# Gate products of a recurrent layer: rounded halves and rests in place of plain float32

## The reference, cut to what matters

```
xb = xc.reshape(b, s, 16, 128)                            # xc: the convolution's output, 2048 wide
r = sigmoid(einsum('bshc,hce->bshe', xb, w_a) + b_a)      # one 128x128 matrix per block
i = sigmoid(einsum('bshc,hce->bshe', xb, w_x) + b_x)
log_a = -8.0 * r * softplus(-lam)
a = exp(log_a)
u = sqrt(-expm1(2.0 * log_a)) * (i * xb)
h[t] = a[t] * h[t-1] + u[t]                               # forward, and once more backward
y = (h_forward + h_backward) * silu(gate) @ w_out + x
```

## Time and profile before

| | |
|---|---|
| median of 3 runs | 2190.18 us (2187.08 to 2191.71) |
| profiled execution | 2186.75 us |
| its span in the trace | 2184.9 us, 29571 instructions |
| granted TensorE clock | 0.995 of full speed |
| recurrent layer, tall panels | 422.4 to 641.5 us |

### The profile page before, as it was taken

One profiled execution on the slowest core, in us unless ns is written; L12 is line 12 of the kernel. 1 busy time (PEld: TensorE's weight loads), 2 busy tenths in 40 slices (PEclk: granted clock), 3 DMA queues, 4 the chain that ended last, 5 costly groups with the idle time before them and its releaser, 6 DMA issues.

```text
span 2184.9 us, 29571 instructions
## 1 busy us (share of the span) xinstructions
PE 2123.9 (97%) x12238; PEld 1521.8 (70%) x12238; DVE 1211.1 (55%) x1983; ACT 855.5 (39%) x1385; POOL 221.1 (10%) x301
## 2 busy tenths in 40 slices
PE   7999999999999999999999999999999899999998
PEld 6868757877777777898888888888867433333333
DVE  3532972439888867875423466345443445544454
ACT  4325461468886544672332542334443111111112
POOL 2000000013331022562000000000001000000000
PEclk9999999999999999999999999999999999999999
DMA  7122112423322444201222221433446899999994
GB/s 249 59 74 93 46 39 83 127 87 97 97 77 94 164 127 154 92 22 41 94 80 97 97 97 40 135 108 123 135 174 243 330 420 420 420 420 420 421 420 194
DMA packets 115703, 366.60 MB, mean 168 GB/s; under 512 B 7952, under 2 KB 36944, under 8 KB 90352
## 3 DMA queue, kind: packets, MB, share of 16 engines
q1 hardware_dynamic: 105888, 329.34, 40.2%
q0 software_dynamic: 9168, 29.00, 3.9%
q10 hardware_dynamic: 512, 6.34, 0.7%
HBM read 358.44 MB, written 10.54 MB: 169 GB/s over the span
## 4 chain that ended last, share of the span: by engine, by line
PE 88%; DVE 8%; ACT 2%; issue 1%; DMA 0%; POOL 0%; SPq 0%; DVEq 0%; ACTq 0%; POOLq 0%
PE bank L956 39%; PE bank L1167 13%; PE bank L1711 10%; PE bank L1725 5%; PE bank L1733 3%; PE bank L1284 2%; PE bank L1180 2%; PE bank L1211 2%; DVE resid L3369 2%; PE bank L1276 1%; PE bank L1113 1%; PE bank L1701 1%; PE bank L1104 1%; DVE w_lo L2447 1%; PE bank L1073 1%
## 5 line engine op out<-in xcount | busy, mean ns | idle before, releaser
L2447 DVE TENSOR_TENSOR w_lo<-raw,w_hi 128x2048 fp32r<-128x2048 f32 x117 | 268.6, 2296 | 444.1 <-ACT w_hi L1842 443.9
L1842 ACT ACTIVATE w_hi<-raw 128x2048 fp32r<-128x2048 f32 x117 | 223.9, 1914 | 393.9 <-PE bank L956 357.5
L3369 DVE TENSOR_TENSOR resid<-bank,resid 128x512 f32<-128x512 f32 x244 | 151.1, 680 | 182.6 <-PE bank L1733 182.6
L956 PE MATMUL bank<-hT_hi,w_hi 128*128 128x512 f32 x512 | 199.9, 390 | 2.5 <-DVE y_lo L3065 2.3
L956 PE MATMUL bank<-hT_lo,w_hi 128*128 128x512 f32 x512 | 199.2, 389 | 0.0
L956 PE MATMUL bank<-hT_hi,w_lo 128*128 128x512 f32 x512 | 199.2, 389 | 0.0
L1711 PE MATMUL bank<-piece,xT 128*64 128x512 f32 x792 | 183.4, 592 | 0.0
L1167 PE MATMUL bank<-hT_hi,w_hi 128*128 128x512 f32 x432 | 173.9, 402 | 0.9 <-DVE hT_lo L2511 0.9
L1167 PE MATMUL bank<-hT_hi,w_lo 128*128 128x512 f32 x432 | 168.2, 389 | 0.0
L1167 PE MATMUL bank<-hT_lo,w_hi 128*128 128x512 f32 x432 | 168.1, 389 | 0.0
L1711 PEld LDWEIGHTS bank<-piece,xT 128*64 128x64 f32 x792 | 59.5, 137 | 118.8 <-issue 118.8
(11 more groups left out here) (625 smaller groups left out, 4166.8 us busy)
## 6 DMA issues: line engine op xcount, KB each, us to landing
piece<-expert_w_gate SPq DMA_DIRECT2D x52, 1024.0 KB, 19.0
piece<-expert_w_down SPq DMA_DIRECT2D x49, 1024.0 KB, 19.2
piece<-expert_w_up SPq DMA_DIRECT2D x47, 1024.0 KB, 20.6
raw<-w_in SPq DMA_DIRECT2D x40, 1024.0 KB, 5.1
raw<-even_w_in SPq DMA_DIRECT2D x18, 1024.0 KB, 5.2
raw<-odd_w_in SPq DMA_DIRECT2D x16, 1024.0 KB, 5.6
raw<-expert_w_gate SPq DMA_DIRECT2D x12, 1024.0 KB, 16.8
raw<-expert_w_up SPq DMA_DIRECT2D x12, 1024.0 KB, 18.9
```

Source lines behind the costliest of these rows:

```text
L956: mm = pe.matmul(out, st, mv, start=first and x == 0, stop=last and x == 2)
L1842: act.activation(split_to(m)[0][:], raw[n % RAW][:], ACT.Copy).then_inc(sem("hi_done"), 1)
L2447: dve.tensor_tensor(split_to(m)[1][:], raw[split_of[m] % RAW][:], f32(split_to(m)[0][:]), ALU.subtract).then_inc(sem("lo_done"), 1)
L3369: dve.tensor_tensor(r, psum[bank][:], r, ALU.add).then_inc(sem(name), 1)
```

## The change

The gates' operands are split into a rounded half and a rest, as those of the large products are, and each plain product becomes three products that add into the same bank. GpSimd makes the four tiles of a block: it copies `gate_w` and `xc` into tiles of the rounded type (128x512 each) and then subtracts these from the originals. There is one set of tiles. So GpSimd waits until the gates of the block before are done on TensorE. It splits block `b + 1` ahead of its products L814 of block `b`. TensorE's two waits (for VectorE's convolution and for the weights' landing) move to GpSimd, and TensorE waits for the subtractions instead.

```diff
+        "gate_hi": ("qkT_done", 3 * NT),
+        "gate_lo": ("qkT_act", 2 * NT),
...
+    gw_hi = nc.alloc_sbuf_tensor_at("gw_hi", [P, 2, 2, P], F32R, offset=free_at)
+    gw_lo = nc.alloc_sbuf_tensor_at("gw_lo", [P, 2, 2, P], F32R, offset=free_at + 2048)
+    xc_hi = nc.alloc_sbuf_tensor_at("xc_hi", [P, SEQ], F32R, offset=free_at + 4096)
+    xc_lo = nc.alloc_sbuf_tensor_at("xc_lo", [P, SEQ], F32R, offset=free_at + 6144)
...
+        def split_gate(blk):
+
+            pool.wait_ge(sem(f"gates_in{blk % 2}"), 32 * (blk // 2 + 1))
+            src = panels[pn["xr"][blk // 2]]
+            pool.wait_ge(sem("evac_dve"), src["at"] + blk % 2 + 1)
+            if blk:
+                pool.wait_ge(sem("gate_done"), 4 * blk)
+            pool.tensor_copy(gw_hi[:], gate_w[blk % 2][:]).then_inc(sem("gate_hi"), 1)
+            pool.tensor_copy(xc_hi[:], xc[:, blk % XC]).then_inc(sem("gate_hi"), 1)
+            pool.wait_ge(*after("gate_hi", 2 * blk + 2))
+            pool.tensor_tensor(gw_lo[:], gate_w[blk % 2][:], f32(gw_hi[:]), ALU.subtract).then_inc(sem("gate_lo"), 1)
+            pool.tensor_tensor(xc_lo[:], xc[:, blk % XC], f32(xc_hi[:]), ALU.subtract).then_inc(sem("gate_lo"), 1)
+
         gate_weights(0)
         gate_weights(1)
+        split_gate(0)
         for blk in range(RB):
+            if blk + 1 < RB:
+                split_gate(blk + 1)
             for it in (2 * blk, 2 * blk + 1):
                 pool.wait_ge(sem("gate_sig"), 2 * it + 2)
                 pool.tensor_tensor(ri[:, it % 8], ri[:, it % 8], xc[:, blk % XC], ALU.mult).then_inc(sem("ix"), 1)
...
         def gates(blk):
 
-            src = panels[pn["xr"][blk // 2]]
-            pe.wait_ge(sem("evac_dve"), src["at"] + blk % 2 + 1)
-            pe.wait_ge(sem(f"gates_in{blk % 2}"), 32 * (blk // 2 + 1))
+            pe.wait_ge(*after("gate_lo", 2 * blk + 2))
...
-                    pe.matmul(psum[n % 4][:], gate_w[blk % 2][:, g, d], xc[:, blk % XC], start=True, stop=True).then_inc(sem("gate_done"), 1)
+                    products = ((gw_hi, xc_hi), (gw_lo, xc_hi), (gw_hi, xc_lo))
+                    for x, (w, v) in enumerate(products):
+                        mm = pe.matmul(psum[n % 4][:], w[:, g, d], v[:], start=x == 0, stop=x == 2)
+                    mm.then_inc(sem("gate_done"), 1)
```

## The result

The changed kernel takes 2198.69 us (median of six runs, 2197.17 to 2200.55) against 2191.4 us for the kernel before in the same sequence (six runs, 2187.08 to 2191.9). The ratio is 1.0038, with a 95% interval of 1.0026 to 1.0049: 0.38% slower, 8.3 us, between 5.7 and 10.7; the two medians lie 7.3 us apart. The forecast was +4.1 us and 2194.3; the range to 2202 holds the time. The 64 runs of before that were made beside the experiments fall into two groups with none between them, 2186.1 to 2188.3 us at a granted clock of 0.995 to 0.997 and 2189.7 to 2192.2 us at 0.993 or 0.994, and the profiled execution of before (2186.75 us) is of the quicker one.

The account below looks back on a forecast made before the run. TensorE was taken to bound the kernel, VectorE 10% behind. VectorE's 18.5 us of losses less 13.6 of waits and head start delay `rp_lo` 4.9 us, the projection 4.1: median 2194.3 us, range 2183 to 2202.

Parts of the forecast that it names:

- Gates cost 2.72 us a block: On TensorE, twelve rounded products take 2.72 us a block instead of 3.43, gaining 9.2 us over blocks 0 to 12.
- TensorE does not wait for the split: On GpSimd, weights' landing and split take 8.7 us, within the tall panel's 10.89 us, with 2 us to spare.
- A two-input instruction of GpSimd costs VectorE 0.97 us; three in four of the splits' hit: On VectorE, splits of blocks 5 to 13: 13.5 subtraction hits at 0.97 us lose 13.1 us.
- Copies: On VectorE, 13.5 hits by GpSimd's copies at 0.4 us lose 5.4 us; a copy alone takes 0.7 us.
- The waits are filled: VectorE's 10.8 us of waits between 504 and 645 us are used up by its 18.5 us of losses.
- The head start: VectorE gains 2.8 us by the round's third convolution, from the faster gates of blocks 0 to 3.
- TensorE loses its lead for `w_lo` of the fourth panel: In the recurrent layer TensorE stalls for VectorE's `w_lo` before a round's fourth panel, which eats its 9.2 us gain.
- The tail costs nothing more: Behind the projection's start, the splits of blocks 14 and 15 add nothing to the +4.1 us.
- Rival 1: Few splits hit VectorE; up to 5.2 us of losses are hidden and the end comes 9.2 us earlier; chance 0.27.
- What contends with what: VectorE instructions with two SBUF inputs block against GpSimd ones that read SBUF; those with at most one don't.

Follow-up runs that it names:

- e2: Changed kernel with GpSimd's splits and TensorE's wait for them, but the plain gate products of the kernel before: 2199.0 us, ratio 1.0046 to before.
- e9: Changed kernel with the whole split on GpSimd, but plain products and no wait of TensorE for the split: 2200.3 us, ratio 1.0052 to before.
- e7: Changed kernel plus seven plain products of constants on TensorE ahead of the output projection: 2195.2 us, ratio 1.0032 to before.
- e1: Changed kernel with only block 0 split on GpSimd; all blocks' gates use those tiles in twelve products: 2183.6 us, ratio 0.9972 to before.

## Why the prediction was right, and by how much its terms were off

**Gates cost 2.72 us a block.** Right, in every block of after that doesn't wait. That a plain product shows as two records doesn't give its price by itself: such a record costs 0.429 us of the beat and the one of a rounded product 0.227. What TensorE does within a record no run here opens.

**TensorE does not wait for the split.** Nearly: 1.4 us once, in the round where the weights' landing held GpSimd for 3.4 us. e2 and e9 make it irrelevant.

**A two-input instruction of GpSimd costs VectorE 0.97 us; three in four of the splits' hit.** The count came out, 13 long hits more against 13.5, but with luck: the subtractions made about 10 of the 20 that they could, half and not three in four, and the old products made 17 in place of 14. The price was low: 14.3/13 = 1.10 us, since hits on `w_lo` and on the floor cost 1.09. This and the count together are 14.3 us for 13.1, the first mis-sized term.

**Copies.** 21 instructions lengthened by 0.29 us, 6.0 us, for a forecast of 13.5 by 0.4, 5.4. A copy alone takes 0.61 us, in the bounds and below the 0.7 taken. The prediction's estimate of 0.43 us beside a start of 0.18 makes just these 0.61; it isn't so that the sum would be the same by it, since 13.5 x (0.61 - 0.31) is 4.1 us and not 5.4. More instructions met a copy than were counted, and each lost less; in no kernel of the table without copies is there a short loss. Losses together: 20.3 us for 18.5. What a hit costs is in every kind the undisturbed length of GpSimd's instruction less 0.2 to 0.3 us (0.61 and 0.29, 1.03 and 0.72, 1.28 and 0.97 to 1.10), which is how the prediction had priced the copies.

**The waits are filled.** Right: 10.9 us down to none. The head start was 1.8 us for 2.8. With the losses this makes `rp_lo` 6.8 us later for 4.9.

**TensorE loses its lead for `w_lo` of the fourth panel.** Right that the lead is eaten, wrong in where. It waited 0.6 us for `w_lo` in the tall panels; 4.2 went in waits for ScalarE to free the gates' banks and 1.4 for the split. Most of it, 9.4, it spent in one wait at the end, for `rp_lo`.

**The tail costs nothing more.** This step failed in the profiled pair. I had taken TensorE's speed after a wait as given. The clock fell in that one long wait, and the distance from the projection's first start to that of the unit in the earlier trace rows grew from 51.18 to 52.60 us (1.4 us). Yet a full clock there would not have brought it back: in e7 the same distance is 53.08 us, because TensorE then waits for VectorE's next `rp_lo` and the second unit runs in a dip. The 3.6 us behind the projection go with a clock that is low for longer, and whether the change is the cause stays open: e1 has them without a long wait, and the runs of before alone spread over 6 us. Added to 4.1: 1.9 at the start of `rp_lo`, 1.2 because that piece was itself held (1.76 us for the 0.68 of the earlier trace rows), 1.4 in the first units, 3.6 behind, together 12.2 of the profiled pair. Between the medians it is 7.3 us, and the 7.2 at the projection's start are the part of the account that the experiments show.

**Rival 1's ceiling.** "Everything is hidden and the end is 9.2 us earlier" would not have come either: e1, without splits, reached 8.2 us at the projection's start (638.04) and 6.6 at the second unit of the earlier trace rows (690.80 for 697.37), because VectorE's own bound lies just below.

**What contends with what.** The hits show it by kind: memsets take nothing, copies a little, two-input instructions most. The Trainium skill, SBUF — State Buffer, "Who interferes with whom", says that two SBUF inputs on VectorE contend with a GpSimd instruction that reads, not with one that only writes. The traces agree. It excepts VectorE's faster modes, and says that `tensor_scalar` can be in one and can then contend; the prediction left that exception out. The floor L2717, a `tensor_scalar` with one input (2048 elements in 1.22 us), was held for 1.09 us.

## What to carry to other kernels

Before moving work to an idle engine, count what the instructions of its neighbour lose beside it, and compare the sum with the neighbour's real waits at the place where it is needed, not with its idle share: here 20 us of lengthening, part of it by GpSimd's old work that now ran at other times, met 11 us of waits, in a stage where the engine showed 10% free. A faster leading engine is worth only the distance to the next bound, and a leader that waits in one piece may come back at a lower clock, but keeping its clock up bought nothing up to the projection's end here (e7), where VectorE was the next to be waited for. On GpSimd one-input copies and memsets are cheap beside a busy VectorE and two-input instructions are dear; the ledger of lengthened instructions shows it in one trace.

## What the runs showed of the hardware that was not expected

- The hold depends on what GpSimd reads: 128x512 memsets none, a copy to the rounded type 0.23 to 0.40 us, a subtraction of one tile from itself 0.72, of two tiles 0.97 to 1.10.
- Without the copies in between, the same subtractions hit more often: 33 for 27 long hits.
- The granted clock was at half (0.50 to 0.52) from 646 us on, 2 us into TensorE's wait of 9.4 us, and still at the first products behind it, which ran at 0.43 us each and not at 0.23.
- From the projection's last product to the end the same program takes 1442.6 to 1448.8 us over the 14 traces, least where the clock doesn't dip in the first 300 us (e7) and most where it is low for 14 us (e1). What decides between these, no run here settles.
